# A mixture-of-experts kernel on one core: places 2 to 13 for 64 tokens, 14 to 27 for 96, 28 to 30 for 64, where 64 and 96 stood in turn

## The chip, the cores and the metric

The kernel runs on one core of one Trainium2 chip. Times are microseconds (us) on the device, of one execution from start to end. In the profile an execution has a span, from its first to its last instruction, and its own time, which is a little longer than the span.

## What is computed

A decoder layer over 512 tokens of width 1024, in float32. A mixer comes first (a gated linear attention and a dilated attention, with their projections). After it each token goes to 4 of 32 experts:

```python
logits = (xn @ router_w + router_b)
top_v, top_e = lax.top_k(logits, TOP_K)          # 4 of 32
gates = jax.nn.softmax(top_v, axis=-1)
...
h = xb @ w_gate_up[e] + b_gate_up[e]             # 1024 -> 2048
gate = jnp.minimum(h[:, ::2], SWIGLU_LIMIT)
up = jnp.clip(h[:, 1::2], -SWIGLU_LIMIT, SWIGLU_LIMIT)
act = (up + 1.0) * (gate * jax.nn.sigmoid(SWIGLU_ALPHA * gate))
return act @ w_down[e] + b_down[e]               # 1024 -> 1024
...
return rmsnorm(h, norm_final_g)
```

The weights of one expert are 8 MB of `w_gate_up` and 4 MB of `w_down`. Each is read from memory once, so the 32 experts bring 384 MB into the core.

## The kernel before, in words

The mixer and the routing take the first 700 us or so. The change doesn't touch them. The rest is the stage of the experts, in which the 32 experts are worked off one after the other, each at a **place** from 0 to 31.

**Sizes.** A place has room for 96 tokens (three groups of 32) or for 64 (two groups). `GROUPS_AT[p]` holds the number of groups at place p, and it is fixed when the program is built. All instructions on TensorE, VectorE, ScalarE and GpSimd that work for a place are cut to its size. Places 0, 1 and 31 have 96 slots and a fixed expert. For places 2 to 30 `order_experts` sorts the 29 other experts on the device by how many tokens chose them: the 14 with the most tokens go to the places of 96, the 15 others to the places of 64. Tokens beyond the room of their expert are left for a loop of further blocks behind the stage (`further_blocks`). In this text a place of 96 is a large one, a place of 64 a small one.

**Bodies.** The program is written out in bodies e = 0 to 30 (`over_bodies`). On TensorE body e does the first product (gate and up) of place e+1, from 8 chunks of weights of 1 MB each (`gate_up_chunk`, line 2023), and then the second product (down) of place e, from 4 chunks (`down_chunk`, line 2032). Between the chunks of gate and up stand two transposes of the activations of place e (`turn_act`, line 1996; the second one only for a large place) and two batches that add the results of place e-1 to the totals (`sum_rows`, line 1967). Between the chunks of down the rows of place e+2 are turned (`turn_rows`, line 1985) and its bias is put in (line 2016).

**Chunks.** The 384 chunks of weights go through a ring of 13 buffers (`expert_chunk`, `expert_chunk_late`). SyncE issues them in order (`load_chunk`, line 1779). Chunk c may be issued when TensorE has used chunk c-13, and TensorE waits for a chunk before it uses it:

```python
def load_chunk(self, sp, c, src):
    r = c % self.RING
    sp.dma_start(self.expert_ring[r][:], src).then_inc(self.chunk_loaded[r], 16)
...
if c >= RING:
    sp.wait_ge(S["used"], c - RING + 1)
```

So at most 13 chunks are in flight or loaded and not yet used. The chunks are the same for a large and a small place; only what TensorE does with each differs. Beside them a body brings three small loads of bias rows (line 1773, SyncE) and the gather of the rows of place e+2 (`gather`, line 1831, GpSimd), of 96 or 64 rows of 4 KB, of which rows of empty slots are skipped.

**Behind the stage** come the last place's down product (`last_down_chunk`, line 2040), the sums, the last norm and the stores.

Of the kernel before, what the change touches and what calls it, by code (L numbers as in the profile page):

```python
# [47 lines left out]
FIRST_SLOTS = 96  # L48
FEW_SLOTS = 64
ORDERED = slice(2, N_EXPERTS - 1)  # L50
N_ORDERED = ORDERED.stop - ORDERED.start
GROUPS_AT = tuple((FEW_SLOTS if p in range(ORDERED.start, ORDERED.stop) and (p - ORDERED.start) % 2 == 0 else FIRST_SLOTS) // 32
                  for p in range(N_EXPERTS))
GROUPS_BEFORE = tuple(sum(GROUPS_AT[:p]) for p in range(N_EXPERTS + 1))
N_FEW = sum(n * 32 == FEW_SLOTS for n in GROUPS_AT)
N_MANY = N_ORDERED - N_FEW
# [17 lines left out]
def shape_constants():  # L74
# [40 lines left out]
    for p in range(ORDERED.start, ORDERED.stop):  # L115
        if GROUPS_AT[p] * QUARTER == FEW_SLOTS:
            order.append(N_MANY + few)
# [39 lines left out]
class Kernel:  # L157
# [1667 lines left out]
    def gather(self, pool, e, u, first=False):  # L1825
        pool.wait_ge(self.moe["index"], e + 1)
        if not first:
            pool.wait_ge(self.moe["x_turned"], 2 * e)
        at = slice(0, GROUPS_AT[e] * QUARTER)
        pool.sem_inc(self.moe["passed"], 1)  # L1830
# [50 lines left out]
    def experts(self, stack):  # L1881
        nc, t = self.nc, self.t
        E, GU, BODY, RING = N_EXPERTS, self.GU, self.PER_BODY, self.RING
        G, PARTS, PIECE, Q = self.GROUPS, self.PARTS, self.PIECE, QUARTER
        GROUPS, BEFORE = GROUPS_AT, GROUPS_BEFORE
        rows, y, a = (self.h[:, b, :] for b in range(3))
# [742 lines left out]
```

## Time and profile before

| what | value |
|---|---|
| median of 3 runs | 1739.06 us (1738.86 to 1740.23) |
| profiled execution, own time | 1741.1 us |
| profiled execution, span | 1739.2 us |
| TensorE busy | 1693.4 us, 97% of the span |
| VectorE, ScalarE, GpSimd busy | 673.1, 361.5, 71.3 us |
| mean traffic of the DMA engines over the span | 283 GB/s |
| traffic from 1029 to 1091 us | 402 GB/s |

The profile counts an engine as busy while it works on an instruction. TensorE's weight loads (PEld) overlap its matmuls (PE). The DMA share is the mean busy share of the core's 16 DMA engines. The ends of matmuls are modelled, so a short wait can hide in a matmul that looks a little longer. One float32 matmul of the program is two records in the trace, so a chunk of 12 matmuls shows as x24. Of 36,172 instructions some matmul records are missing, which shows in counts such as x18 or x20 for a batch of 24 matmuls in `sum_rows`; the durations of stretches are not touched by it.

### The profile page before, as it was taken

The numbers are of one execution on the slowest core, as the hardware profiler recorded it, in microseconds if no ns is written. First come the engines' busy times: TensorE is split into PE (matmuls) and PEld (weight loads), VectorE is DVE, ScalarE is ACT, GpSimd is POOL, SyncE is SP. The second block draws the span as 40 slices with busy tenths as digits, with TensorE's granted clock in tenths as the row PEclk, the third lists the DMA queues.
The fourth block names the chain that finished last, engine by engine and source line by source line (L and its number), as shares of the span: only waits on it lengthen the run. The fifth ranks groups of instructions, "written<-read, shape, count | busy, mean of one in ns | idle before, by whom it ended". The sixth has DMA issues, their size and how long they took to land.

```text
span 1739.2 us, 36172 instructions
## 1 busy us (share of the span) xinstructions
PE 1693.4 (97%) x15794; PEld 984.1 (57%) x15795; DVE 673.1 (39%) x1060; ACT 361.5 (21%) x643; POOL 71.3 (4%) x89
## 2 busy tenths in 40 slices
PE   9999999999999999999999999999999999999997
PEld 7887778898888885344444344343344343344344
DVE  4247355527333453334234333332332332332434
ACT  4244322227532231110101101011011011011011
POOL 1000000000000004100000000000000000000000
PEclk9999999999999999999999999999999999999999
DMA  5422164421232397899999999999999999999991
GB/s 191 134 73 73 37 200 121 121 79 38 98 107 96 136 355 285 332 399 383 398 405 401 400 408 394 407 408 392 405 409 395 406 405 396 404 404 393 404 372 60
DMA packets 97402, 492.37 MB, mean 283 GB/s; under 512 B 12592, under 2 KB 14832, under 8 KB 47648
## 3 DMA queue, kind: packets, MB, share of 16 engines
q1 hardware_dynamic: 92416, 479.42, 71.3%
q0 software_dynamic: 3776, 8.54, 1.7%
q10 hardware_dynamic: 1056, 2.16, 0.6%
q8 instruction: 120, 1.97, 0.5%
q14 instruction: 34, 0.28, 0.0%
HBM read 480.20 MB, written 8.96 MB: 281 GB/s over the span
## 4 chain that ended last, share of the span: by engine, by line
PE 41%; DMA 13%; SPq 6%; issue 1%; DVE 1%; ACT 0%; POOL 0%; DVEq 0%
PE psum L2023 23%; PE psum L2032 11%; DMA expert_chunk<-in_expert_w_down 6%; SPq L1779 5%; DMA expert_chunk<-in_expert_w_gate_up 3%; PE psum L1967 3%; DMA expert_chunk_late<-in_expert_w_down 3%; PE psum L1985 1%; SPq L1773 1%; PE psum L1996 1%; PE psum L2040 1%; PE psum L2016 1%; PE psum L2150 0%; PE psum L281 0%; SPq L1857 0%
## 5 line engine op out<-in xcount | busy, mean ns | idle before, releaser
L2023 PE MATMUL psum<-expert_chunk,rowsT 128*32 128x512 f32 x2896 | 330.9, 595 | 7.0 <-DMA expert_chunk<-in_expert_w_gate_up 6.7
L1978 DVE TENSOR_TENSOR added_rowsT<-added_rowsT,psum 128x512 f32<-128x512 f32 x240 | 148.8, 682 | 390.2 <-PE psum L1967 390.2
L2023 PE MATMUL psum<-expert_chunk_late,rowsT 128*32 128x512 f32 x2096 | 239.8, 595 | 5.4 <-DMA expert_chunk_late<-in_expert_w_gate_up 5.2
L327 DVE TENSOR_TENSOR chunk_lo<-chunk,chunk_hi 128x2048 fp32r<-128x2048 f32 x48 | 110.0, 2291 | 257.2 <-ACT chunk_hi L323 238.8
L2023 PEld LDWEIGHTS psum<-expert_chunk,rowsT 128*32 128x32 f32 x2896 | 86.5, 109 | 199.2 <-issue 175.3
L2032 PE MATMUL psum<-expert_chunk,activationsT 128*32 128x256 f32 x3360 | 190.6, 380 | 3.3 <-DMA expert_chunk<-in_expert_w_down 3.3
L2032 PEld LDWEIGHTS psum<-expert_chunk,activationsT 128*32 128x32 f32 x3360 | 110.3, 110 | 83.3 <-issue 22.2
L358 PE MATMUL psum<-xT_hi,chunk_hi 128*128 128x512 f32 x384 | 150.3, 391 | 4.3 <-DVE chunk_lo L327 1.7
L358 PE MATMUL psum<-xT_hi,chunk_lo 128*128 128x512 f32 x384 | 149.5, 389 | 0.0
L358 PE MATMUL psum<-xT_lo,chunk_hi 128*128 128x512 f32 x384 | 149.5, 389 | 0.0
L2023 PEld LDWEIGHTS psum<-expert_chunk_late,rowsT 128*32 128x32 f32 x2096 | 62.4, 109 | 146.4 <-issue 129.2
L2083 ACT ACTIVATE gate_sigmoid<-gate_values 128x768 f32<-128x768 f32 (+1 forms) x32 | 23.8, 745 | 570.8 <-DVE gate_values L2100 570.8
L323 ACT CAST chunk_hi<-chunk 128x2048 fp32r<-128x2048 f32 x48 | 91.8, 1912 | 190.0 <-PE psum L358 158.0
L1943 DVE SCALAR_TENSOR_TENSOR last_rows_lo<-psum,piece_weight,last_rows_hi 128x256 fp32r<-128x256 f32 x78 | 33.4, 479 | 214.9 <-ACT last_rows_hi L1936 214.9
L358 PE MATMUL psum<-chunk_hi,xT_hi 128*128 128x512 f32 x288 | 113.5, 394 | 2.6 <-ACT gla_v L760 1.5
L358 PE MATMUL psum<-chunk_hi,xT_lo 128*128 128x512 f32 x288 | 112.7, 391 | 0.0
L358 PE MATMUL psum<-chunk_lo,xT_hi 128*128 128x512 f32 x288 | 112.6, 391 | 0.0
L2032 PE MATMUL psum<-expert_chunk_late,activationsT 128*32 128x256 f32 x1632 | 93.0, 380 | 2.0 <-DMA expert_chunk_late<-in_expert_w_down 2.0
L358 PEld LDWEIGHTS psum<-xT_hi,chunk_hi 128*128 128x128 f32 x384 | 72.1, 188 | 20.8 <-DVE chunk_lo L327 2.4
L358 PEld LDWEIGHTS psum<-xT_hi,chunk_lo 128*128 128x128 f32 x384 | 72.1, 188 | 15.2
L358 PEld LDWEIGHTS psum<-xT_lo,chunk_hi 128*128 128x128 f32 x384 | 72.1, 188 | 14.8
L2032 PEld LDWEIGHTS psum<-expert_chunk_late,activationsT 128*32 128x32 f32 x1632 | 53.2, 110 | 41.8 <-issue 11.8
(307 smaller groups left out, 1704.3 us busy)
## 6 DMA issues: line engine op xcount, KB each, us to landing
expert_chunk<-in_expert_w_gate_up SPq DMA_DIRECT2D x152, 1024.0 KB
expert_chunk_late<-in_expert_w_gate_up SPq DMA_DIRECT2D x104, 1024.0 KB
expert_chunk<-in_expert_w_down SPq DMA_DIRECT2D x87, 1024.0 KB
expert_chunk_late<-in_expert_w_down SPq DMA_DIRECT2D x41, 1024.0 KB
chunk<-in_w_in SPq DMA_DIRECT2D x38, 1024.0 KB, 5.1
chunk<-in_w_branch_gla SPq DMA_DIRECT2D x4, 1024.0 KB, 5.1
chunk<-in_w_mix_out SPq DMA_DIRECT2D x4, 1024.0 KB, 5.1
gla_v<-in_x SPq DMA_DIRECT2D x4, 512.0 KB
```

Of the source, the lines that this page charges most:

```text
L323: act.copy(self.whi[c][:], self.raw[c][:]).then_inc(self.hi_done[c], 1)
L327: dve.tensor_tensor(self.wlo[c][:], self.raw[c][:], self.whi[c][:].bitcast(F32), ALU.subtract).then_inc(self.lo_done[c], 1)
L358: last = pe.matmul(bank, stationary, moving, start=(k == 0 and n == 0), stop=(k == KT - 1 and n == 2))
L1773: sp.dma_start(rows[j * QUARTER:j * QUARTER + 2 * self.PARTS, :], self.bias_table[bass.ds(e, 1), :, :, :].rearrange("a m s n -> (a m s) n" ...
L1779: sp.dma_start(self.expert_ring[r][:], src).then_inc(self.chunk_loaded[r], 16)
L1943: dve.scalar_tensor_tensor(out=y_lo[:, at], in0=y_of(j), scalar=self.piece_weight[e % self.BUFFERS][:, j:j + 1], in1=y_hi[:, at].bitcast(F ...
L1967: last = pe.matmul(sum_banks[p], x[part_rows(p), at:at + P], token_hot[part_rows(p), j, :], start=(x is y_hi and j == 0), stop=(x is y_lo ...
L1978: last = dve.tensor_tensor(to, to, sum_banks[p], ALU.add)
L1985: last = pe.transpose(turned(f, e)[:, k, :], rows[slots_of(e), (HALF_KT * f + k) * P:(HALF_KT * f + k + 1) * P], self.ident[slots_of(e), s ...
L2023: last = pe.matmul(bank[part_rows(p), :], x[:, k, part_rows(j)], w[:, p // 2, p % 2 * COLS:(p % 2 + 1) * COLS], start=False, stop=(k == KT ...
L2032: last = pe.matmul(y_of(j)[part_rows(p), :], aT[:, q, kk, part_rows(j)], w[:, kk, p * PIECE:(p + 1) * PIECE], start=(q == 0 and kk == 0), ...
L2083: act.activation(held(sg, e), held(gv, e), ACT.Sigmoid, scale=SWIGLU_ALPHA).then_inc(S["sig"], 1)
```

## The change

The table of sizes is written differently. The numbers of places stay: 15 of 64 slots and 14 of 96 between places 2 and 30, and places 0, 1 and 31 of 96.

```diff
-GROUPS_AT = tuple((FEW_SLOTS if p in range(ORDERED.start, ORDERED.stop) and (p - ORDERED.start) % 2 == 0 else FIRST_SLOTS) // 32
+FEW_PLACES = (*range(2, 14), 28, 29, 30)
+GROUPS_AT = tuple((FEW_SLOTS if p in FEW_PLACES else FIRST_SLOTS) // 32
                   for p in range(N_EXPERTS))
```

Before, the small places were 2, 4, 6, ..., 30. Now they are 2 to 13 and 28 to 30. Lines below the table move down by one, so line 2023 of before is line 2024 of the change. The experts are still sorted by their number of tokens, and the same 14 get 96 slots. The order in which SyncE issues its transfers, and their sizes, stay as they were.

On TensorE, from the start of body 2, before: the names say what is multiplied, `rowsT` are the rows of a place in the first product, `activationsT` those of the second, and the x counts the instructions of a row.

```order
L2023 MATMUL psum<-expert_chunk,rowsT 32x512 x12
L1996 MATMUL psum<-identity_sb,h_sb 128x128 x4
L2023 MATMUL psum<-expert_chunk,rowsT 32x512 x12
L2023 MATMUL psum<-expert_chunk_late,rowsT 32x512 x12
L1967 MATMUL psum<-tokens_one_hot,last_rows_hi 128x512 x12
L1967 MATMUL psum<-tokens_one_hot,last_rows_lo 128x512 x12
L2023 MATMUL psum<-expert_chunk_late,rowsT 32x512 x36
L1967 MATMUL psum<-tokens_one_hot,last_rows_hi 128x512 x12
L1967 MATMUL psum<-tokens_one_hot,last_rows_lo 128x512 x12
L2023 MATMUL psum<-expert_chunk_late,rowsT 32x512 x12
L2023 MATMUL psum<-expert_chunk,rowsT 32x512 x12
L2032 MATMUL psum<-expert_chunk,activationsT 32x256 x32
```

The same place of the program in the change:

```order
L2024 MATMUL psum<-expert_chunk,rowsT 32x512 x8
L1997 MATMUL psum<-identity_sb,h_sb 128x128 x4
L2024 MATMUL psum<-expert_chunk,rowsT 32x512 x8
L2024 MATMUL psum<-expert_chunk_late,rowsT 32x512 x8
L1968 MATMUL psum<-tokens_one_hot,last_rows_hi 128x512 x12
L1968 MATMUL psum<-tokens_one_hot,last_rows_lo 128x512 x12
L2024 MATMUL psum<-expert_chunk_late,rowsT 32x512 x24
L1968 MATMUL psum<-tokens_one_hot,last_rows_hi 128x512 x12
L1968 MATMUL psum<-tokens_one_hot,last_rows_lo 128x512 x12
L2024 MATMUL psum<-expert_chunk_late,rowsT 32x512 x8
L2024 MATMUL psum<-expert_chunk,rowsT 32x512 x8
L2033 MATMUL psum<-expert_chunk,activationsT 32x256 x32
```

The eight chunks of place 3 have 8 matmuls each in place of 12; the four chunks of place 2 that follow have 32 in two, as they had. Up to body 12 all bodies now read so.

The second place is the end of body 15 on TensorE, before, from the fourth chunk of place 16:

```order
L2023 MATMUL psum<-expert_chunk_late,rowsT 32x512 x24
L1967 MATMUL psum<-tokens_one_hot,last_rows_hi 128x512 x8
L1967 MATMUL psum<-tokens_one_hot,last_rows_lo 128x512 x8
L2023 MATMUL psum<-expert_chunk_late,rowsT 32x512 x8
L2023 MATMUL psum<-expert_chunk,rowsT 32x512 x8
L2032 MATMUL psum<-expert_chunk,activationsT 32x256 x48
L1985 MATMUL psum<-identity_sb,h_sb 128x96 x8
L2016 MATMUL psum<-bias_rows,bias_place_r 128x512 x3
L2032 MATMUL psum<-expert_chunk,activationsT 32x256 x48
```

And in the change:

```order
L2024 MATMUL psum<-expert_chunk_late,rowsT 32x512 x36
L1968 MATMUL psum<-tokens_one_hot,last_rows_hi 128x512 x12
L1968 MATMUL psum<-tokens_one_hot,last_rows_lo 128x512 x12
L2024 MATMUL psum<-expert_chunk_late,rowsT 32x512 x12
L2024 MATMUL psum<-expert_chunk,rowsT 32x512 x12
L2033 MATMUL psum<-expert_chunk,activationsT 32x256 x48
L1986 MATMUL psum<-identity_sb,h_sb 128x96 x8
L2017 MATMUL psum<-bias_rows,bias_place_r 128x512 x3
L2033 MATMUL psum<-expert_chunk,activationsT 32x256 x48
```

The chunks of place 16 have 12 matmuls in place of 8, and those of place 15 keep theirs. From body 14 to body 26 all bodies now have both products large.

## Rows read from the trace of the kernel before

**Rows 1.** The page: the span, busy time of each engine, DMA share by slices, a DMA queue

```profile
span 1739.2 us, 36172 instructions
PE 1693.4 (97%) x15794; PEld 984.1 (57%) x15795; DVE 673.1 (39%) x1060; ACT 361.5 (21%) x643; POOL 71.3 (4%) x89
DMA  5422164421232397899999999999999999999991
...
q0 software_dynamic: 3776, 8.54, 1.7%
```

**Rows 2.** Windows: stretch, its length, busy us by engine, TensorE clock, DMA share, GB/s

```profile
1029.00:1091.00 62.00, 62.00 (x755) 26.00 (x749) 21.70 (x38) 6.70 (x16) 1.91 (x2) 1.00 1.02 402
1091.00:1153.00 62.00, 61.92 (x751) 26.45 (x743) 21.50 (x37) 6.70 (x16) 1.91 (x2) 1.00 1.01 402
1153.00:1215.00 62.00, 59.09 (x711) 24.68 (x711) 21.82 (x37) 6.69 (x16) 1.91 (x2) 1.00 1.01 401
1588.00:1650.00 62.00, 60.48 (x731) 25.42 (x723) 18.60 (x35) 6.36 (x16) 1.91 (x2) 1.00 1.01 399
```

**Rows 3.** What TensorE waited for, from 1113.5 to 1698 us: us, times, longest

```profile
PE psum L2023 <- DMA expert_chunk<-in_expert_w_gate_up: 6.7, 10, 1.2
PE psum L2023 <- DMA expert_chunk_late<-in_expert_w_gate_up: 5.2, 7, 1.4
```

**Rows 4.** Windows: gate and up, then down, of body 8; the same of body 9

```profile
956.29:981.09 24.80, 24.80 (x248) 8.54 (x244) 7.36 (x12) 1.85 (x5) 0.00 (x0) 1.00 1.01 407
981.09:989.19 8.10, 8.10 (x142) 4.81 (x138) 3.95 (x7) 1.49 (x3) 0.96 (x1) 1.00 1.01 402
989.19:1006.71 17.52, 17.52 (x171) 5.75 (x166) 6.87 (x11) 1.86 (x5) 0.00 (x0) 1.00 1.02 396
1006.71:1018.45 11.74, 11.74 (x207) 7.02 (x203) 3.64 (x8) 1.49 (x3) 0.95 (x1) 1.00 1.01 407
```

**Rows 5.** The chain in bodies 8 and 9, small pieces: start, us, what

```profile
974.20 1.60 PE psum L1967 x20
...
993.35 0.37 PE psum L1996 x2
...
1002.00 1.14 PE psum L1967 x11
```

**Rows 6.** DMA issues: transfers, count, KB of each

```profile
expert_chunk<-in_expert_w_gate_up SPq DMA_DIRECT2D x152, 1024.0 KB
...
bias_rows<-biases_hi_lo SPq DMA_DIRECT2D x96, 16.0 KB
```

**Rows 7.** The chain: starts of body 2 and body 13, in the order of time

```profile
769.81 2.58 PE psum L2023 x24
...
1113.50 1.72 PE psum L2023 x16
```

**Rows 8.** Timeline of TensorE: the first wait of over 0.1 us for a chunk

```profile
1181.87 1.92 PE L2023 MATMUL psum<-expert_chunk_late,rowsT 128*32 128x512 f32 x16 [1.40 <-DMA expert_chunk_late<-in_expert_w_gate_up]
```

**Rows 9.** The chain: down of body 17, down of body 25, first product behind body 30

```profile
1262.38 5.39 PE psum L2032 x96
...
1523.39 5.39 PE psum L2032 x96
...
1697.98 3.60 PE psum L2040 x8
```

**Rows 10.** Windows of 5 us in the stage: one beside a gather, the quickest

```profile
1015.00:1020.00 5.00, 5.00 (x84) 2.49 (x79) 0.98 (x3) 1.21 (x3) 0.00 (x0) 1.00 1.02 348
...
1095.00:1100.00 5.00, 5.00 (x60) 1.88 (x52) 0.00 (x0) 0.00 (x0) 0.00 (x0) 1.00 1.03 428
```

**Rows 11.** Windows of 5 us ahead of the stage, with the clock last but two

```profile
660.00:665.00 5.00, 5.00 (x16) 4.23 (x17) 3.07 (x11) 1.09 (x3) 1.01 (x2) 0.50 1.02 407
695.00:700.00 5.00, 2.45 (x12) 0.60 (x11) 0.00 (x0) 0.00 (x0) 2.95 (x4) 1.00 0.02 2
```

## The prediction

> **What bounds the kernel now.** The page comes first: TensorE is busy for 97% of the span, and in slices 18 to 39 of the 40 the DMA engines stand at 9 [rows 1]. Both look full in the stage of the experts, so the question is which one waits for the other, and when. The windows of about one pair of bodies answer it [rows 2]. Up to 1091 us TensorE is busy for all of its time. From 1153 us on it has gaps of 1.5 to 2.9 us in 62. The DMA engines are at full share in all four windows, at 399 to 402 GB/s. So the transfers are the slower of the two all along. They start with a lead, and TensorE eats it up. The waits bear this out: behind 1113 us the first product waits for chunks of weights [rows 3], and the first wait of over 0.1 us falls in body 15, at 1181.87 us [rows 8].
>
> **What a body costs TensorE.** Bodies 8 and 9 lie where nothing waits, so their windows are pure work [rows 4]. A large gate and up takes 24.80 us, a small down 8.10, a small gate and up 17.52, a large down 11.74. A pair is 62.16 us, or 31.08 a body. Which piece goes with which size has to be watched at two places: the second transpose of activations, 0.37 us, comes only in a body whose own place is large, and each of the two batches of sums takes 1.60 us for a large place before it and 1.14 for a small one [rows 5]. With that:
> - small body behind a small one: 17.52 - 0.37 + 8.10 = 25.25 us
> - large body behind a large one: 24.80 + 0.37 + 11.74 = 36.91 us
> - the seams: body 2 is 25.25 + 0.92 = 26.17, body 13 (large gate and up, small down, small sums) 24.80 + 8.10 - 0.92 = 31.98, body 14 36.91 - 0.92 = 35.99, body 27 29.26 + 0.92 = 30.18, body 28 26.17, body 29 25.25, body 30 31.98.
>
> **What a body costs the DMA engines.** A body brings 12 transfers of 1024 KB, three of 16 KB and one gather [rows 6]. That is 12.58 + 0.05 MB, and the gather's queue moved 8.54 MB for 32 places [rows 1], 0.27 MB each: 12.90 MB. At the 402 GB/s of the windows this is 32.1 us, whatever the size of the place. The chain gives a second price: from the down of body 17 at 1262.38 us to that of body 25 at 1523.39 [rows 9], where TensorE runs on the transfers' heels, are 8 bodies in 261.01 us, 32.63 each. I take 32.1 for the small stretch, since the gathers there bring fewer rows and a gather costs traffic (348 GB/s in the window beside one, 428 at best [rows 10]).
>
> **The lead.** Before, TensorE needs 31.08 us a body and the transfers 32.63, so a body uses up 1.55 us of lead. From the start of body 2 at 769.81 us [rows 7] to the wait in body 15 are 13 bodies: the lead at body 2 is 13 x 1.55 = 20 us. In the change TensorE will wait at nearly every chunk and not only at the worst one of a pair, so it can come a little closer; I take 21 us. The ring holds 13 chunks of 32.1 / 12 = 2.7 us, one of them in use, so no lead can be above 32 us.
>
> **The change, part by part.** It adds and removes no instruction and no byte: of bodies 2 to 30, before, the work is 14 pairs of 62.16 and a last body of 32.90, 903.1 us, and the change's bodies add up to the same (below). What moves is where TensorE is faster than the transfers.
> 1. Bodies 2 to 12 take 26.17 + 10 x 25.25 = 278.7 us of TensorE, the transfers 11 x 32.1 = 353.1. The lead covers 21. Body 13 can start at 769.81 + 353.1 - 21 = 1101.9 us, where the work alone would have it at 1048.5. TensorE waits 53.4 us here. The cover, the lead, is gone after about three bodies (21 / 6.85).
> 2. Bodies 13 to 30 take 31.98 + 35.99 + 12 x 36.91 + 30.18 + 26.17 + 25.25 + 31.98 = 624.5 us. From body 14 on TensorE is the slower one, by 36.91 - 32.1 = 4.8 us a body, so there is nothing more to wait for but some 1 us at the seam. The transfers build their lead up to the ring's end in 6 or 7 bodies, and in the 6 or 7 bodies after that SyncE has to wait for room: about 6.5 x 4.8 = 31 us of transfer time that nobody uses. This is the same loss seen from the other side.
> 3. Bodies 27 to 29 take 81.6 us of TensorE and 96.3 of the transfers. The 14.7 us come out of the lead of 28 or so, at no cost. Without that lead they would be waits.
> 4. The waits of before go: the first product behind body 30 started at 1697.98 us [rows 9], and 1697.98 - 769.81 - 903.1 leaves 25 us of waiting. Some of it sits inside matmuls that look longer, which is why the wait rows show less.
>
> Nothing is queued behind the waits that someone else needs earlier: the gather of place e+2 starts at TensorE's turn in body e-1 and has a body's time, and VectorE and ScalarE were busy for 35% and 11% of the pair [rows 4], with shorter pieces in the small bodies. The end of the kernel behind body 30 is as it was.
>
> **The sum.** Start of the last down: 1101.9 + 624.5 + 1 = 1727.4 us, against 1697.98: 29.4 us later. The profiled execution took 1741.1 us by its own time, 2.0 above the median of 1739.06, so I put the difference on the median: **1768 us**, 1.7% slower.
>
> **Bounds of the pace.** The one unknown is how fast the transfers go while TensorE hangs on them. With the quickest window's 428 GB/s a body is 30.1 us and the loss 7 us. With the 32.63 of the chain and a lead of 16 us the loss is 40 us. Neither end is near: 428 is a window without a gather, and the small stretch has eleven.
>
> On the quick end the Trainium skill has a ceiling ("DMA: Bandwidth & Descriptors", section "Where 436 GB/s comes from"): 435 GB/s at the ports of SBUF. By an estimate from it a body is 29.7 us at the least and the kernel 3 us slower than before at best. The section's other limit, about 358 GB/s on the side of HBM, is not what this trace shows: 402 GB/s over 62 us.
>
> **Rivals.**
> - *The bytes decide, the order does not.* The DMA engines are at full share from slice 18 to slice 39 [rows 1] and their bytes stay the same. If they never stopped, the time would be 1739. For this the ring would have to hold what 14 large bodies gain, 13 x 4.8 = 62 us, on top of nothing; it holds 32. 5%.
> - *Faster.* If transfers ran quicker while TensorE waits (fewer rows gathered, fewer reads of SBUF by TensorE), the small stretch could shrink. The end stays where it was at a pace of (1072.5 - 769.81 + 21) / 11 = 29.4 us a body, 439 GB/s; at 28.0 us the kernel takes 1723 us. No window is above 428. 4%.
> - *The clock falls.* In the small stretch TensorE works 25.25 of 32.1 us, 79%. The clock was at 0.50 from 660 to 665 us, which is 1.2 GHz, and at 1.00, 2.4 GHz, from 695 to 700 with TensorE busy for 2.45 of 5 us [rows 11], so gaps alone don't decide it. At 1.2 GHz a small body would take 50.5 us, 18.4 above the transfers. If half of the eleven bodies ran so, that is 101 us more: 1869 us. A clock that is low for less than a quarter of the time would hide in the waits. 5%.
>
> The Trainium skill speaks for this last rival ("TensorE: Matmul & The Clock Gate", section "HAM oscillation — how this bites in real kernels"): waits for a DMA between bursts of matmuls send the clock back to half rate. Before, the waits for chunks did not: the clock is 1.00 in all of rows 2.
>
> **The numbers.** The forecast, waits in the small stretch and full buffers in the large one, has 86%, and in nearly all of it the loss is above 3.5 us. 0.2% is 3.5 us, about what a measurement of this kernel can tell from no change. Faster by more: 4%, the second rival. Within: 5%. Slower by more: 91%. The range is 1757 to 1778: a pace of 31.1 us (415 GB/s) at the low end, 32.6 with a lead of 17 at the high one. It leaves out the rivals and the ends of the bounds.
>
> **What would show it.** The DMA share stays at full up to about 1350 us, at some 402 GB/s. From about 750 to 1100 us, and from 850 on above all, TensorE is busy for about 79% and waits for chunks in the first product and in down, some 50 us in all. Body 13 starts at about 1102 us. From there to about 1610 us TensorE has no gap, and from about 1370 us on the traffic falls to 12.90 MB / 36.91 us = 350 GB/s. No waits for chunks at the end. I am wrong if the small bodies come every 30 us or less, if the clock leaves 1.00 in the stage, or if the traffic never falls before the end.

## The result, and the profile after

| | before | changed |
|---|---|---|
| median | 1738.96 us (1737.35 to 1740.23, 4 runs) | 1772.79 us (1769.48 to 1773.25, 3 runs) |
| profiled execution, own time | 1741.1 us | 1772.79 us |
| its span | 1739.2 us | 1771.0 us |
| last down | 1697.98 us [rows 9] | 1729.64 us |

The kernel is slower: the ratio is 1.0184 with an interval of 1.0169 to 1.0199, which is 32.0 us on 1738.96. A fourth run of the changed kernel, of 2447.0 us, had a mean TensorE clock of 0.653 of full speed where the others had 0.99; it has no trace, so what held its clock down stays open, and it is in no comparison.

The page of the changed kernel, with the lines that answer to [rows 1]; GB/s by slices of 44 us is added:

```profile
span 1771.0 us, 36172 instructions
PE 1700.5 (96%) x15794; PEld 979.3 (55%) x15795; DVE 673.9 (38%) x1060; ACT 361.3 (20%) x643; POOL 70.9 (4%) x89
...
PE   9999999999999999999888888999999999999997
DMA  5321254421324397999999999999999999999991
GB/s 191 128 86 57 73 163 121 118 73 38 119 95 143 122 392 281 370 400 404 395 407 401 403 408 396 405 406 401 391 376 353 358 346 346 355 347 378 401 418 57
```

The page nearly tells it alone. TensorE drops to 8 in slices 20 to 25 of the 40, 841 to 1107 us, with the traffic at 400 GB/s. Then it is at 9, and in slices 31 to 36 (1328 to 1594 us) the traffic falls to 346 to 358 GB/s. The row of DMA digits shows none of this: a share of 0.95 still prints as 9. The bytes per second have to be read beside it.

Windows of the changed kernel, columns as in [rows 2]: two in the small stretch, one body of it, the fall of the clock, one large body, two later ones:

```profile
904.00:966.00 62.00, 50.77 (x568) 18.41 (x557) 20.11 (x36) 4.88 (x12) 0.93 (x1) 1.00 1.01 403
1029.00:1091.00 62.00, 52.47 (x568) 19.02 (x564) 17.73 (x31) 4.89 (x13) 1.92 (x2) 0.97 1.01 402
...
873.75:906.18 32.43, 26.83 (x303) 9.98 (x303) 10.08 (x19) 2.78 (x8) 0.93 (x1) 1.00 1.01 402
...
1040.00:1045.00 5.00, 4.54 (x28) 1.23 (x32) 0.00 (x0) 0.00 (x0) 0.00 (x0) 0.66 1.01 401
...
1208.50:1245.55 37.05, 37.05 (x454) 15.66 (x449) 11.84 (x19) 3.93 (x9) 0.96 (x1) 1.00 1.01 399
...
1463.00:1525.00 62.00, 62.00 (x743) 25.55 (x735) 15.68 (x27) 6.15 (x15) 1.75 (x2) 1.00 0.95 350
1649.00:1711.00 62.00, 62.00 (x733) 25.27 (x729) 22.52 (x38) 5.74 (x14) 0.96 (x1) 1.00 1.01 411
```

In the small stretch TensorE is busy for 50.77 of 62 us, 82%, where the trace of before had 62.00 and 61.92 [rows 2]. The transfers go at 402 to 403 GB/s in both kernels. So TensorE's waiting did not make them faster. From 1463 us on it is the other way round: TensorE has no gap and the traffic is 350 GB/s.

What TensorE waited for in the changed kernel from 739 to 1143 us (us, times, longest):

```profile
PE psum L2024 <- DMA expert_chunk<-in_expert_w_gate_up: 19.1, 26, 1.8
PE psum L2024 <- DMA expert_chunk_late<-in_expert_w_gate_up: 12.4, 13, 2.0
PE psum L2033 <- DMA expert_chunk_late<-in_expert_w_down: 5.9, 11, 0.7
PE psum L2033 <- DMA expert_chunk<-in_expert_w_down: 4.7, 7, 1.5
```

Together that is 42.1 us in 57 waits. From 1143 to 1711 us the same view has none for a chunk. TensorE's timeline at body 6, at the next body, around 1040 us and at body 13 (start, us, engine, line, operation, operands; in brackets the idle time ahead of it):

```profile
873.75 1.93 PE L2024 MATMUL psum<-expert_chunk,rowsT 128*32 128x512 f32 x16 [0.63 <-DMA expert_chunk<-in_expert_w_gate_up]
875.60 0.66 PE L1997 MATMUL psum<-identity_sb,h_sb 128*128 128x128 f32 x4
878.03 1.92 PE L2024 MATMUL psum<-expert_chunk,rowsT 128*32 128x512 f32 x16 [1.77 <-DMA expert_chunk<-in_expert_w_gate_up]
880.59 1.92 PE L2024 MATMUL psum<-expert_chunk,rowsT 128*32 128x512 f32 x16 [0.64 <-DMA expert_chunk<-in_expert_w_gate_up]
...
906.18 1.93 PE L2024 MATMUL psum<-expert_chunk,rowsT 128*32 128x512 f32 x16 [0.64 <-DMA expert_chunk<-in_expert_w_gate_up]
...
1040.46 5.34 PE L2024 MATMUL psum<-expert_chunk_late,rowsT 128*32 128x512 f32 x32 [2.03 <-DMA expert_chunk_late<-in_expert_w_gate_up]
...
1046.87 3.64 PE L2024 MATMUL psum<-expert_chunk,rowsT 128*32 128x512 f32 x32
...
1100.82 2.78 PE L2024 MATMUL psum<-expert_chunk_late,rowsT 128*32 128x512 f32 x24 [0.64 <-DMA expert_chunk_late<-in_expert_w_gate_up]
1105.27 4.93 PE L2024 MATMUL psum<-expert_chunk_late,rowsT 128*32 128x512 f32 x44 [1.08 <-DMA expert_chunk_late<-in_expert_w_gate_up]
```

A small chunk is 1.9 us of matmuls, and the next chunk comes 2.6 us after the one before it. The rest is a wait of 0.64 us. From 873.75 to 1100.82 us are seven bodies, 32.44 us each. The small bodies no longer run at the pace of their work, which was put at 25.25 us, but at that of the transfers.

The chain of the changed kernel: the start of body 2, three large bodies, the last down.

```profile
767.52 1.72 PE psum L2024 x16
...
1208.50 2.57 PE psum L2024 x24
...
1245.55 2.58 PE psum L2024 x24
...
1282.59 2.58 PE psum L2024 x24
...
1729.64 3.60 PE psum L2041 x8
```

A large body takes 37.05 us. The other side of the loss shows among SyncE's waits. The view of waits from 720 to 1700 us, of the changed kernel (what waits, for what; us, times, longest):

```profile
SPq L1780 <- PE psum L2024: 309.8, 134, 3.8
SPq L1780 <- PE psum L2033: 175.2, 77, 6.1
```

The same of the kernel before:

```profile
SPq L1779 <- PE psum L2023: 207.0, 107, 3.8
SPq L1779 <- PE psum L2032: 99.0, 55, 3.5
```

SyncE waits for room 485.0 us in place of 306.0. Not all of that stops the transfers, since several chunks are still in flight while it waits for room for one more, so the sum can't measure the loss. The quickest kernel of this study, the one with a single bias load below, has even more of it in the same stretch:

```profile
SPq L1779 <- PE psum L2023: 389.6, 192, 6.0
SPq L1779 <- PE psum L2032: 206.2, 103, 8.9
```

The traffic measures it better. In slices 31 to 36 it is 351 GB/s on average in place of 403. By an estimate from that, 266 us x (1 - 351/403) = 34 us of transfer time go unused there.

### The profile page after: what moved, and what is told of

It reads as the page before. It is cut to its first block, busy times and chain, and to the rows that moved or that the text cites. A ratio compares the mean times of both kernels' runs of the same rounds, so it can differ in the third digit from the quotient of the medians.

```text
span 1771.0 us, 36172 instructions
## 1 busy us (share of the span) xinstructions
PE 1700.5 (96%) x15794; PEld 979.3 (55%) x15795; DVE 673.9 (38%) x1060; ACT 361.3 (20%) x643; POOL 70.9 (4%) x89
## 2 busy tenths in 40 slices
DMA packets 97402, 492.37 MB, mean 278 GB/s; under 512 B 12592, under 2 KB 14832, under 8 KB 47648
## 4 chain that ended last, share of the span: by engine, by line
PE 40%; SPq 13%; DMA 5%; issue 2%; DVE 1%; POOL 1%; ACT 0%; DVEq 0%; POOLq 0%
PE psum L2024 22%; SPq L1780 12%; PE psum L2033 11%; PE psum L1968 4%; DMA expert_chunk_late<-in_expert_w_gate_up 2%; DMA expert_chunk<-in_expert_w_gate_up 2%; SPq L1774 1%; PE psum L1997 1%; PE psum L1986 1%; PE psum L2041 1%; PE psum L2017 1%; POOL slots_of_experts L1813 1%; DMA h_sb<-normed_rows,row_index 0%; DMA slots_of_experts<-choice_token_and_weight,choice_row_of_table 0%; PE psum L2151 0%
## 5 line engine op out<-in xcount | busy, mean ns | idle before, releaser
L2024 PE MATMUL psum<-expert_chunk_late,rowsT 128*32 128x512 f32 x2096 | 240.6, 598 | 12.6 <-DMA expert_chunk_late<-in_expert_w_gate_up 12.4
L2033 PEld LDWEIGHTS psum<-expert_chunk,activationsT 128*32 128x32 f32 x3360 | 106.7, 110 | 89.3 <-issue 21.8
## 6 DMA issues: line engine op xcount, KB each, us to landing
expert_chunk<-in_expert_w_gate_up SPq DMA_DIRECT2D x152, 1024.0 KB, 12.4
```

The costliest lines, as they stand in the source:

```text
L2024: last = pe.matmul(bank[part_rows(p), :], x[:, k, part_rows(j)], w[:, p // 2, p % 2 * COLS:(p % 2 + 1) * COLS], start=False, stop=(k == KT ...
L2033: last = pe.matmul(y_of(j)[part_rows(p), :], aT[:, q, kk, part_rows(j)], w[:, kk, p * PIECE:(p + 1) * PIECE], start=(q == 0 and kk == 0), ...
```

## The experiments

Each kernel was timed beside the kernel before on the same chip. A change of so many us is worked out from the ratio. The runs answer four questions.

### Is it the length of a run of equal places?

Four kernels differ from the changed one in one line, the set of the small places:

```diff
-FEW_PLACES = (*range(2, 14), 28, 29, 30)
+FEW_PLACES = tuple(p for p in range(2, 31) if (p - 2) // 2 % 2 == 0)   # twos
+FEW_PLACES = tuple(p for p in range(2, 31) if (p - 2) // 5 % 2 == 0)   # fives
+FEW_PLACES = tuple(range(2, 17))                                       # fifteen first
+FEW_PLACES = tuple(range(16, 31))                                      # large first
```

> Small places 2, 3, 6, 7, 10, 11, ... 30: two and two. Theory of the lead (a run of small places costs only what it draws beyond the lead that the ring holds): two small bodies draw 2 x 7 = 14 us of a lead of 20, and two large ones give 2 x 4.7 back, so this is the kernel before: 1739 us, within 4. Rival, the seams (each change between 64 and 96 costs something): half as many seams as before, a time below before's by some us, about 1730. Rival, bytes decide: 1739 as well.

> Small places 2 to 6, 12 to 16, 22 to 26. Theory of the lead: prices now taken from the changed kernel's trace, 7.15 us drawn by a small body and 4.64 given by a large one. Five small bodies draw 36 us: of the first lead of 21 some 10 us of waits are left, then 23 us are rebuilt and 13 lacking, twice. Waits of about 38 us against 25 before: 1752 us, 1748 to 1757. Rival, bytes decide: 1739. Rival, each small body next to a small one costs the same (34 us for 13 such pairs in the change, 2.6 each): 12 pairs, 1770.

> All 15 small places first (2 to 16), then the 14 large ones. Theory of the lead: 14 bodies x 7.15 = 100 us drawn, 21 covered, 79 us of waits against 25: 1793 us, 1788 to 1798. It also says what the three small places at the end were worth in the change, about 20 us. Rival, seams: one seam fewer than the change, not slower than 1773. Rival, the end needs small places for another reason: a long wait behind body 29.

> The mirror: large places 2 to 15, small ones 16 to 30. Theory of the lead: the ring is full after two large bodies (20 grows to 30), SyncE waits for room through the rest of them, and the 15 small bodies draw 107 us of which 28 are covered: 79 us of waits against 25, 1793 us, 1786 to 1799, and the transfers at 350 GB/s in the first half and not in the second. Rival, it is the small places' standing first that costs (a lead not yet built): then the mirror is near 1739. Rival, bytes decide: 1739.

| order of sizes | median us | before | ratio | us |
|---|---|---|---|---|
| twos | 1739.80 | 1741.38 | 0.999 [0.9974, 1.0006] | -1.7 |
| fives | 1754.78 | 1741.38 | 1.0088 [1.0059, 1.0116] | +15.3 |
| fifteen small ones first | 1797.07 | 1741.38 | 1.0328 [1.0301, 1.0354] | +57.1 |
| fourteen large ones first | 1795.66 | 1741.38 | 1.0314 [1.0283, 1.0345] | +54.7 |

Windows of fives, at the end of its first run of small places, then of the kernel with fifteen small ones first (its small and its large stretch), then of the one with the large ones first (large and small):

```profile
842.00:904.00 62.00, 56.76 (x637) 21.30 (x641) 18.81 (x31) 5.57 (x14) 1.95 (x2) 1.00 1.01 401
```

```profile
904.00:966.00 62.00, 51.42 (x562) 18.39 (x558) 20.13 (x36) 4.98 (x12) 1.52 (x2) 0.97 1.01 402
...
1525.00:1587.00 62.00, 62.00 (x723) 25.04 (x719) 17.56 (x30) 6.15 (x15) 0.96 (x1) 1.00 0.95 354
```

```profile
904.00:966.00 62.00, 62.00 (x784) 27.22 (x780) 21.22 (x34) 7.49 (x17) 1.92 (x2) 1.00 0.93 351
...
1525.00:1587.00 62.00, 51.17 (x572) 18.84 (x568) 19.25 (x34) 4.69 (x12) 1.88 (x2) 1.00 1.01 405
```

The longer the runs, the slower, and all four times lie within what was expected of the lead. In fives the waits come where the lead must have run out: TensorE is busy for 58.53 of 70 us from 1140 us on and for 53.53 of 65 from 1470 on, but for all of the 255 and 260 us before each, while five large places build the lead up again. Twos have half the seams of the kernel before and take the same time, so seams cost nothing that shows. Fifteen small ones in a row cost about the same at the front as at the end. The two stretches only swap places: 51 of 62 us busy where the places are small, 350 GB/s where they are large. The price is thus in the bookkeeping between the two paces.

### Do the transfers set the pace?

If so, both orders should take the same time once the transfers are fast. From chunk 13 on each transfer brings half of its chunk, so the products use stale numbers for the other half; the work of every engine stays as it was.

```diff
-        sp.dma_start(self.expert_ring[r][:], src).then_inc(self.chunk_loaded[r], 16)
+        part = slice(0, 1 if c >= self.RING else 2)
+        sp.dma_start(self.expert_ring[r][:, part, :], src[:, part, :]).then_inc(self.chunk_loaded[r], 16)
```

> The changed order, but from chunk 13 on each transfer brings only the first half of its chunk (4 KB of 8 KB a partition), so the products use old weights in the other half: the output is not the reference's, the instructions on all engines are the same. Theory of the lead: transfers of 6.3 MB a body take about 16 to 17 us, TensorE never waits for a chunk, and the time is the work alone: 1739 - 25 = 1714 us, 1710 to 1718, and within 3 us of the same edit of the order before. Rival, a run of small places costs TensorE in itself (clock, seams, late gathers): it stays about 30 us above the order before with the same edit.

> The order before with the same halved transfers (output not the reference's). Theory of the lead: no waits, 1739 - 25 = 1714 us, 1710 to 1718. Rival: the 25 us that I call waits are something else, and the time stays at 1739.

The changed kernel with half transfers takes 1711.33 us (ratio 0.9825 [0.9808, 0.9843]), the kernel before with them 1712.12 (0.9834 [0.9817, 0.9851]). The 32 us between the orders are gone. The window at 904 us and the one wait of TensorE left in the stage, changed order:

```profile
904.00:966.00 62.00, 62.00 (x782) 26.93 (x782) 26.75 (x48) 6.80 (x17) 2.80 (x3) 1.00 0.83 264
...
PE psum L1998 <- DVE h_sb L2112: 0.5, 1, 0.5
```

From body 2 at 764.20 us to the last down at 1667.95 are 903.75 us, where the prediction worked out 903.1 us of work. The order before gives up 29 us, 4 more than its 25 us of waits. Body 2 started at 761.69 us there, 8 us earlier than in [rows 7], and from there to the last down (1665.34) are 903.65 us. So transfers seem to cost something ahead of body 2 too, which the prediction did not count. How much is not shown: in the eleven kernels with whole transfers and a small place 2 it starts anywhere from 765.09 to 773.47 us.

### Is it the ring's depth that covers a run?

Both kernels again with nine chunks in place of 13 between SyncE and TensorE (the same line in two places; the buffers stay):

```diff
-                sp.wait_ge(S["used"], c - RING + 1)
+                sp.wait_ge(S["used"], c - 9 + 1)
```

> The order before, with SyncE waiting until chunk c-9 is used in place of c-13: four chunks fewer ahead. Theory of the lead: the lead at body 2 is four chunks shorter, 4 x 2.7 = 11 us, and nothing else changes since a pair draws only 2.5: 1750 us, 1746 to 1754. Rival, the DMA engines need more transfers in flight to run at full rate: a pace above 32.6 us a body all along, over 1760.

> The changed order with nine chunks ahead. Theory of the lead: 11 us less lead for the first small bodies, and a ring that holds 21 us in place of 32, of which the last small places need 15: 1773 + 11 = 1784 us, up to 1789 if the end runs short. Rival, as for the order before: far above 1790.

The kernel before takes 1749.74 us (1.0048 [1.0034, 1.0063], +8.4 us), the changed one 1785.56 (1.0255 [1.0238, 1.0273], +44.4 us, 12.4 more than with 13). Four chunks at 2.7 us are 10.8 us of lead, and each order loses about that. The profiled executions show it more closely: from body 2 to the last down are 938.1 us in place of 928.2, and 973.1 in place of 962.1, so 9.9 and 11.0 us more. The lead shrinks with the ring, chunk for chunk. For a deeper ring this follows only by extension: no run had one.

### What sets the pace of 32.4 us a body?

By bytes, at 402 GB/s, the gather of a place is 0.7 us of it and the three bias loads 0.1 us. Two kinds of kernels measured the price. In the first, the gathers from place 2 on bring one row of 4 KB, so the products work on stale rows:

```diff
+        if e >= 2:
+            pool.dma_start(self.h[0:1, 0, :], self.normed[0:1, :]).then_inc(self.moe["gathered"], 16)
+            return
```

In the second, each of the three bias loads of a body brings one row of 2 KB in place of eight, from place 2 on, which leaves out part of the bias:

```diff
+            if u >= 2:
+                sp.dma_start(rows[j * QUARTER:j * QUARTER + 1, :],
+                             self.bias_table[bass.ds(e, 1), 0:1, 0:1, :].rearrange("a m s n -> (a m s) n")
+                             ).then_inc(self.bias_in[u % 2], 16)
+                continue
```

> The order before; the gathers of places 2 to 31 are replaced by a transfer of one row, so TensorE works on old rows (output not the reference's, same instructions on TensorE, VectorE, ScalarE). A body brings 12.63 MB in place of 12.90. If only the bytes of a gather count, its pace goes from 32.63 to 31.9 us and the waits from 25 to about 13: 1727 us. If a gather also slows the transfers beside it (the dips to 325 to 355 GB/s in windows of 5 us), the pace is 12.63 MB at 415 to 423 GB/s, 29.9 to 30.4 us, under TensorE's 31.08, and the waits are gone: 1714 us. Rival, the pace has nothing to do with gathers: 1739.

> The changed order with the same edit (output not the reference's). In the small stretch the bodies come at the pace of the transfers: 31.7 us if only bytes count (11 x 0.7 = 8 us less than the change, 1765), 29.9 to 30.4 if a gather slows its neighbours (22 to 27 us less, 1746 to 1751). Either way it stays slower than the same edit of the order before, by 27 us or more, since 30 us is still above the 25.25 of a small body. Rival, pace independent of gathers: 1773.

> The order before; each of the three loads of bias rows of a place from 2 on brings one row of 2 KB in place of eight (biases wrong in the output). 0.04 MB of 12.90 a body: by the bytes 0.1 us a body and 3 us in all, 1736 to 1739, not to be told from no change. Rival, these small transfers, like the gathers, cost more than their bytes: a pace of 32 us or less and 1725 or below.

| kernel | median us | before | ratio | us |
|---|---|---|---|---|
| no gathers, order before | 1719.22 | 1743.56 | 0.9857 [0.984, 0.9873] | -24.9 |
| no gathers, changed order | 1757.93 | 1743.56 | 1.0078 [1.0057, 1.01] | +13.6 |
| one bias row a load, order before | 1729.51 | 1743.56 | 0.9923 [0.9905, 0.994] | -13.4 |

TensorE's timeline of the changed order without gathers, at the first transposes of bodies 7 and 13, and a window between them:

```profile
903.11 0.66 PE L2000 MATMUL psum<-identity_sb,h_sb 128*128 128x128 f32 x4
...
1089.39 0.66 PE L2000 MATMUL psum<-identity_sb,h_sb 128*128 128x128 f32 x4
...
904.00:966.00 62.00, 53.29 (x604) 19.86 (x596) 20.13 (x36) 5.21 (x14) 0.97 (x2) 1.00 1.01 415
```

The same two places of the changed order with its gathers:

```profile
908.03 0.66 PE L1997 MATMUL psum<-identity_sb,h_sb 128*128 128x128 f32 x4
...
1103.53 0.66 PE L1997 MATMUL psum<-identity_sb,h_sb 128*128 128x128 f32 x4
```

Six bodies in 186.28 us are 31.05 us each, at 415 GB/s, and in 195.50 us 32.58 each. So a gather costs 1.53 us of the pace. In these six bodies the gather's queue moved 1.54 MB with the gathers, 0.26 MB each, which is 0.64 us at 403 GB/s: the price is more than twice the bytes. The pace lies between what was expected if only bytes count (31.7) and if a gather slows its neighbours (29.9 to 30.4). In the order before the gathers' absence takes away all waits: from body 2 at 772.19 us to the last down at 1675.84 are 903.65 us, the bare work. The 24.9 us saved are thus a lower bound of their price there. In the changed order +32.0 us became +13.6, 18.4 us, of which 11 bodies of 1.53 us are 16.8. On 1738.96 us the ratio gives 1752.5, a little above what was expected of it.

The bias loads were the miss of the study. By their bytes they can bring 3 us: 21 rows of 2 KB left out for each of 30 places are 1.3 MB, 3.2 us at 402 GB/s. It measured 13.4, and the profiled execution has the saving behind body 2: 914.3 us from there to the last down in place of 928.2. The theory of bytes fell for them, and the rival that small transfers cost more than their bytes stood.

That pointed to a version that computes all that the reference asks. The three loads bring the same eight rows to three groups of partitions, for three matmuls that put the bias in. One load is enough, if all three matmuls read it:

```diff
-        for j in range(self.GROUPS):
+        for j in range(1):
...
-            pe.wait_ge(self.bias_in[e % 2], 16 * G * (e // 2 + 1))
+            pe.wait_ge(self.bias_in[e % 2], 16 * (e // 2 + 1))
...
-                pe.matmul(bank, self.bias_place[part_rows(j), :], self.bias_rows[e % 2][part_rows(j), :].bitcast(F32R),
+                pe.matmul(bank, self.bias_place[part_rows(0), :], self.bias_rows[e % 2][part_rows(0), :].bitcast(F32R),
```

> The order before, all of the reference computed: the bias rows of a place are loaded once and not three times, and the two or three bias matmuls all read the first copy. If the three small loads cost more than their bytes on the slowest DMA engine, as the run with one row each showed (0.77% or 13.4 us for 7 of 8 rows of 3 loads, 21 rows, 0.64 us a row over the kernel), 16 rows less give 16 x 0.64 = 10 us: 1729 us at a before of 1739, a ratio of 0.994, 0.992 to 0.996. Against it: the bias matmuls now follow each other on TensorE, by about 0.2 to 0.4 us a body, which stays under the pace of the transfers. Rival: it was the number of rows on one load that counted, or wrong biases changed something else; then the ratio is 1.000.

With the order before it takes 1731.51 us (1728.65 to 1734.33, five runs), ratio 0.9947 [0.9933, 0.996], 9.2 us less than before: quicker than both kernels and inside the expected 0.992 to 0.996. Its chain and the windows that answer to the last two of [rows 2]:

```profile
953.97 0.89 PE psum L2016 x3
...
1687.72 3.60 PE psum L2040 x8
...
1153.00:1215.00 62.00, 62.00 (x747) 26.28 (x743) 21.82 (x37) 6.50 (x16) 1.91 (x2) 1.00 1.01 404
...
1588.00:1650.00 62.00, 61.30 (x718) 25.50 (x714) 22.01 (x35) 6.69 (x16) 0.96 (x1) 1.00 1.01 409
```

The three bias matmuls take 0.89 us of the chain, 0.43 before, so the saving is net of that. TensorE has no gap at 1153 us, where it had 2.9. The traffic is 404 and 409 GB/s, and the last down starts 10.3 us earlier, though body 2 starts 1.8 us later (771.65). By rows the two bias kernels agree: 13.4 us for 21 rows less in each body, 9.2 us for 16, which is 0.64 and 0.58 us a row over the kernel.

## Why the prediction was right, point by point

- **What bounds the kernel.** Right. Halving the transfers makes both orders equal, at the predicted work to within 1 us (903.75 for 903.1).
- **Start of body 2.** It stood at 769.81 in the sum and came at 767.52. These 2.3 us lie ahead of the ordered places. The other kernels with whole transfers and a small place 2 start it from 765.09 to 773.47 us, so chance is enough for them; no run shows that it was chance.
- **Small stretch.** Body 13 was to start 332.1 us after body 2 and did 333.3 after it (1100.82 - 767.52). That is 54.6 us of waiting over the 278.7 of work; 53.4 was said. TensorE was busy for 82% against 79%, since part of the waits hides in matmuls: the wait rows show 42.1. The lead covered three bodies, as said: the first transposes of bodies 3, 4 and 5 start at 795.20, 820.30 and 845.42 us, 25.1 apart, and that of body 6 at 875.60.
- **One term of the work.** The second transpose was put at 0.37 us, its piece in the chain. With 0.51 the measured bodies come out: 24.80 + 0.51 + 11.74 = 37.05 for a large one (36.91 was said) and 17.52 - 0.51 + 8.10 = 25.11 for a small one (25.25 was said). The sum over all bodies does not feel it, since the change moves the term from one side to the other.
- **Pace and lead.** Two errors cancel, and that is luck. The pace was 32.44 and not 32.1, which is 3.7 us over eleven bodies. The lead used was 11 x 32.44 - 333.3 = 23.5 us and not 21, which gives 2.5 back. The pace was put at 12.90 MB over 402 GB/s. The traffic was as said, 403 GB/s, but the bodies came slower: 12.90 MB in 32.44 us are 398 GB/s. The kernel before had the same gap, 12.90 MB in 32.63 us or 395 GB/s beside 402, and the prediction took the quicker price because small places gather fewer rows. That was not enough of a reason: the small stretch kept nearly all of the gap. No run settles what makes it.
- **From body 13 to the last down.** 625.5 was said, 628.8 measured. A large body takes 0.14 us more than said, 1.7 us over twelve bodies. The seam has gaps of 1.08 us at 1105.27 and 0.95 at 1141.52, where 1 was counted.
- **The sum.** 29.4 - 2.3 + 1.2 + 3.3 = 31.6 us, and the last down moved by 31.66. The median came 5 us above the forecast, inside the range.
- **The lead comes back to nothing.** Right: 350 GB/s from 1463 us on, no wait for a chunk from 1143 to 1711 us, and some 34 us of transfer time unused, by the estimate above, where 31 was said.
- **The rival of bytes alone** is out, by the orders. **The faster rival** is out too: the transfers stayed at 402 to 403 GB/s while TensorE waited. Even without gathers they went at 415, where 439 was needed.
- **The rival of the clock** showed itself and cost nothing visible in the runs compared. The prediction called itself wrong if the clock left 1.00 in the stage, and it did: on this point it failed, though the time did not feel it. From 1041.0 to 1044.5 us the granted clock was 0.50, 1.2 GHz, after bodies with 18% of idle time; the window of 62 us around it has 0.97. The timeline above shows why the time hardly felt it: behind a wait of 2.03 us two chunks took 5.34 us in place of 3.64, and nothing was waited for behind them. The transfers take 2 x 2.7 us for two chunks in any case, so the dip took the place of waits. The Trainium skill's rule ("TensorE: Matmul & The Clock Gate", section "HAM oscillation — how this bites in real kernels") has waits for a DMA send the clock back to half rate; here this happened once in eleven bodies. In windows of 5 us behind body 2, such falls stand in the traces of all the orders that wait much: once in fives, in large ones first and in the changed order without gathers, twice in fifteen small ones first, three times in the changed order with nine chunks. In twos, in the order before and its variants, and in both kernels with half transfers there is none up to the last down. Why it falls behind one wait and not behind another stays open.

## What to carry to other kernels

Where tiles of unlike work share a ring of equal transfers, compare the two paces one size at a time, not their mean. A run of n tiles that are quicker than their transfers costs n times the difference less the lead, and a run of slow ones gives back no more than the ring holds. Alternate as long as the lead is short, and look for the loss in bytes per second, stretch by stretch, since a busy share hides it and the producer's waits for room do not measure it. When the transfers are the bound, price the small ones beside them by leaving them out: their bytes are no measure.

## What the hardware showed that was not expected

- **Small loads cost four times their bytes.** Leaving out 21 rows of 2 KB a body saved 13.4 us where the bytes are 3.2 us. The Trainium skill has a rule that bears on it ("DMA: Bandwidth & Descriptors", section "Rules for kernel authors"): a transfer whose outermost dimension is smaller than 16 uses at most as many engines. By an estimate from it, eight rows load half of the 16 engines and double the price, to 6.4 us. That is half of what was measured. The packet counts fit the eight: the kernel with one bias load issues 64 loads less, and its trace has 12,080 packets of under 512 B in place of 12,592, eight for each. Which engines carry the rows, and where the other half of the price comes from, no run here shows.
- **A gather costs more than twice its bytes**, 1.53 us for 0.26 MB, beside transfers that run at full rate.
- **The transfers did not speed up when TensorE waited**: 402 and 403 GB/s with TensorE busy for 100% and for 82%. So its reads of SBUF were no burden on them that shows.
- **The clock fell to 0.50 for 3.4 us** in a stretch of short waits, and it fell in every order with long stretches of waits, up to three times in one execution, and in no order without them.
